# A two-layer trunk with a mixture of experts: the scatter moved into each expert, in four row tiles, and a shorter TensorE program for groups without second token blocks

## The reference

```
g_p, g_idx = top_k(softmax(x @ wg + bg), 1)
e_in       = logits of the 8 experts of that group
top_v, top_i = top_k(e_in, 2);  gate = g_p * softmax(top_v)
for expert e and its tokens:      # w1, w3: (1024, 512), w2: (512, 1024), float32
    a = silu(xb @ w1[e]) * (xb @ w3[e])
    y[tokens] += (a @ w2[e]) * gate
```

## Time and profile before

| | |
|---|---|
| runs | 1131.81, 1134.48, 1135.38 us |
| profiled execution | 1131.81 us, span 1130.0 us |
| mean granted TensorE clock | 0.928 of full |
| busy: PE, PEld, DVE, ACT | 880.1, 511.3, 345.5, 232.5 us |
| HBM read over the span | 423.85 MB, 376 GB/s |
| the chain that ended last | DMA 44%, PE 41%, DVE 7%, issue 5%, ACT 2% |

### The profile page before, as it was taken

How to read it: one execution, slowest core, us unless ns; L and a number is a source line. 1 busy time by engine, 2 the same in 40 slices (tenths; PEclk the granted TensorE clock), 3 DMA queues, 4 the chain that set the end, 5 groups by cost and what they waited for, 6 DMA issues and landing times.

```text
span 1130.0 us, 19738 instructions
## 1 busy us (share of the span) xinstructions
PE 880.1 (78%) x8032; PEld 511.3 (45%) x8033; DVE 345.5 (31%) x821; ACT 232.5 (21%) x559; POOL 4.6 (0%) x14
## 2 busy tenths in 40 slices
PE   6878777677786778589999988787887676768766
PEld 5644434333443344344886554443544343334433
DVE  2523222321322223222366253231332222213314
ACT  2421111110211111112144322110221121102112
POOL 1000000000000000000000000000000000000000
PEclk9899989998998989899999999999998898989979
DMA  9999999999999999998405459999999999999992
GB/s 299 428 424 424 425 426 425 423 427 425 426 425 426 425 426 426 425 425 358 176 1 200 166 208 426 425 426 413 426 426 425 425 426 425 428 423 425 427 426 112
DMA packets 33478, 427.19 MB, mean 378 GB/s; under 512 B 4706, under 2 KB 5986, under 8 KB 7988
## 3 DMA queue, kind: packets, MB, share of 16 engines
q1 hardware_dynamic: 33028, 424.19, 89.2%
q0 software_dynamic: 304, 0.72, 0.4%
HBM read 423.85 MB, written 1.05 MB: 376 GB/s over the span
## 4 chain that ended last, share of the span: by engine, by line
DMA 44%; PE 41%; DVE 7%; issue 5%; ACT 2%; DVEq 0%; SPq 0%
DMA ring<-in_moe_w 43%; PE ps L457 14%; PE ps L493 6%; PE ps L631 5%; PE ps L510 3%; PE ps L613 2%; DVE work L1061 2%; PE ps L411 2%; PE ps L685 2%; PE ps L363 1%; DMA work<-in_consts 1%; DVE work L1069 1%; ACT work L791 1%; PE ps L389 1%; DVE work L1063 1%
## 5 line engine op out<-in xcount | busy, mean ns | idle before, releaser
L457 PE MATMUL ps<-ring,work 128*32 128x256 f32 x4224 | 298.2, 434 | 164.8 <-DMA ring<-in_moe_w 100.7
L457 PEld LDWEIGHTS ps<-ring,work 128*32 128x32 f32 x4224 | 165.8, 124 | 304.7 <-issue 210.0
L1059 DVE TENSOR_SCALAR work<-work 128x128 f32<-128x128 f32 (+1 forms) x64 | 14.6, 229 | 501.3 <-ACT work L791 501.3
L493 PE MATMUL ps<-ring,work 128*32 128x256 f32 x2112 | 127.5, 382 | 30.8 <-DVE work L1069 30.2
L411 PE MATMUL ps<-work,h_sb 128*128 128x256 f32 (+1 forms) x576 | 136.2, 380 | 4.5 <-issue 3.8
L1095 DVE COPY hT<-ps 32x512 f32<-32x512 f32 x128 | 87.4, 683 | 149.0 <-PE ps L493 148.1
L791 ACT ACTIVATE work<-ps 128x256 f32<-128x256 f32 x64 | 24.5, 383 | 510.2 <-PE ps L457 510.2
L411 PEld LDWEIGHTS ps<-work,h_sb 128*128 128x128 f32 x576 | 99.6, 190 | 42.8 <-issue 32.9
L493 PEld LDWEIGHTS ps<-ring,work 128*32 128x32 f32 x2112 | 62.9, 109 | 92.9 <-DVE work L1069 44.9
L799 ACT COPY hT<-ps 32x512 f32<-32x512 f32 x128 | 73.9, 577 | 123.6 <-PE ps L493 122.9
L764 ACT ACTIVATE work<-ps,gcol 128x256 f32<-128x256 f32 (+1 forms) x144 | 58.6, 458 | 110.7 <-PE ps L411 110.7
(11 more groups left out here) (146 smaller groups left out, 420.8 us busy)
## 6 DMA issues: line engine op xcount, KB each, us to landing
ring<-in_moe_w SPq DMA_DIRECT2D x192, 2048.0 KB, 30.4
ring<-in_attn_wv SPq DMA_DIRECT2D x2, 2048.0 KB, 33.0
ring<-in_attn_wq SPq DMA_DIRECT2D x2, 2048.0 KB, 32.0
ring<-in_attn_wk SPq DMA_DIRECT2D x2, 2048.0 KB, 34.0
ring<-in_attn_wo SPq DMA_DIRECT2D x2, 2048.0 KB, 37.1
x_sb<-in_x SPq DMA_DIRECT2D x2, 512.0 KB, 5.7
work<-in_pool_w SPq DMA_DIRECT2D x1, 1024.0 KB, 13.0
out_x<-h_sb SPq DMA_DIRECT2D x2, 512.0 KB, 2.6
```

The costliest lines, as they stand in the source:

```text
L457: mm = pe.matmul(gu_ps[SB * j:SB * (j + 1), b, :, :], xg[:, u, kt, b, k, :], w[:, :, kt, P * j:P * (j + 1)], start=(kt == 0 and b == 0), s ...
L493: mm = pe.matmul(y_ps[SB * i:SB * (i + 1), b, :], actT[:, b, SB * j:SB * (j + 1)], w[:, j, 256 * i:256 * (i + 1)], start=(j == 0 and b == ...
```

## The change

The scatter is done after each expert's down products, by eight products per block: 32 rows deep (one expert's tokens stand in four copies, one for each quarter of the 1024 columns, at the partitions where the down products put them), 256 columns wide, four row tiles of PE, each with its own PSUM bank. `y` is then copied whole (128x256 for each block), by VectorE alone, and the gates are spread fourfold and transposed for each expert. The result lies in the banks by quarters of the columns, so that the residual is one instruction of 1024 columns for each half of the tokens. Banks of layer 1's first transposes and value products are moved, with which two waits of the queries go.

For each group TensorE now reads the largest count of tokens first and takes one of two programs: one for groups with no second block, without any branch within, and one as before. For the first group of a round the short one stands first, for the second group the long one.

More of the change, by code:

```diff
@@ L64 @@
 C_ALL = C_BAND + len(WINDOWS) * BW
-FILL_LAST = 1
 FILL_NEXT = 3
@@ L436, in group, with blocks_of_group @@
             def group(s, g, u, placed, rounds, fullest, tokens, chunk):
+                most = fullest()
[11 more added lines that the diff above has]
+                        blocks_of_group(s, g, u, placed, rounds, 1, lambda k: None, chunk)
+            def blocks_of_group(s, g, u, placed, rounds, blocks, tokens, chunk):
                 def second_block(count, step):
+                    if blocks == 1:
+                        return
                     if count is None:
@@ L1077, in group @@
                 ve.wait_ge(s["onehot"], placed)
-                for t in range(TH):
-                    ins = ve.tensor_tensor(gated[:, t, :, :, :], onehot[:, u, t, :, :, :],
-                                           W[:, t, bass.ds(gl * E4, E4)].unsqueeze(1).unsqueeze(3).to_broadcast([P, NB, E4, SB]),
-                                           ALU.mult)
-                ins.then_inc(s["gated"], 1)
                 for k in range(E4):
                     n1 = g * E4 + (k + 1)
+                    for t in range(TH):
+                        ins = ve.tensor_tensor(gated[:, t, :, :, :],
+                                               onehot[:, u, t, :, k, :].unsqueeze(2).to_broadcast([P, NB, 4, SB]),
+                                               W[:, t, bass.ds(gl * E4 + k, 1)].unsqueeze(1).unsqueeze(3)
+                                               .to_broadcast([P, NB, 4, SB]), ALU.mult)
+                    ins.then_inc(s["gated"], 1)
                     count = tokens(k)
@@ L1121, in experts, with residual @@
                                     group(fb, m * NGRP + g, g, u, m * (NGRP + 1) + g + 1, lambda k: None, lambda k: 0)
-                                    ve.wait_ge(fb["sc"], ACC * (m * NGRP + g + 1))
-            def residual(t, done, before):
+                                    ve.wait_ge(fb["sc"], E4 * (m * NGRP + g + 1))
+            def residual(t):
                 for i in range(2):
-                    ve.wait_ge(done, before + 2 * t + i + 1)
+                    ve.wait_ge(s_wo, 2 * t + i + 1)
                     xs = x_sb[:, t, 512 * i:512 * (i + 1)]
@@ L1163, in _ @@
             for t in range(TH):
-                residual(t, main["sc"], ACC * (NGRP - 1))
+                expert_residual(0, t)
                 copy_hT(1, t)
@@ L1241, in _ @@
             for t in range(TH):
-                residual(t, s_wo, 0)
+                residual(t)
                 copy_hT(2, t)
@@ L1248, in _ @@
             for t in range(TH):
-                residual(t, main["sc"], ACC * (2 * NGRP - 1))
+                expert_residual(1, t)
             for t in range(TH):
```

52 lines of the change are left out of this document (16 added, 36 removed).

## The result

| | before | after |
|---|---|---|
| median | 1133.22 us (4 runs) | 1146.37 us (1143.88 to 1146.85, 4 runs) |
| ratio, 95% interval | | 1.0114 [1.0102, 1.0126] |
| profiled execution, span | 1131.81, 1130.0 | 1146.15, 1144.3 |
| mean granted TensorE clock | 0.928 | 0.903 |

The direction and the range of the forecast (1140, 1129 to 1152) were right; the loss is twice as large as forecast: 14.3 us from profile to profile, where the sum has 7. The page after, against the earlier trace rows: slices of the span, instruction queue, gate products.

The account below looks back on a forecast made before the run. DMA was taken to bound the expert streams. The terms -2.2 - 1.4 + 10 + 0.5 + 0.1 = +7 gave 1138.8 us from the profiled execution, 1141.5 from the median; forecast 1140, range 1129 to 1152.

Parts of the forecast that it names:

- What bounds it: Expert streams: DMA at mostly 425 or 426 GB/s sets the time, hiding TensorE while it frees ring slots soon enough.
- the three open places: Where time is not hidden: end of layer 0, the very end, and start of layer 1, with DMA standing still.
- End of layer 0: Wait for the last scatter before attention: value products start at 508.9 against 511.06, a gain of 2.2 us.
- The end: Last scatter and first residual of the kernel: residual done at 1120.0 against 1121.41, a gain of 1.4 us.
- The ninth expert: Layer 1, behind the group with second blocks: two fetches, gate products end at 795.5, queue stands still 10 us longer.
- Other boundaries: Remaining group ends: double jumps fit, TensorE keeps 6.7 us per iteration; cost 0.5 us, bounds 0 and 8.
- the third rival: Short iterations: both holes follow every jump, TensorE becomes the bound, 10 to 15 us more, 1153 us; chance 0.12.
- The first rival: Group ends: jumps are free or hidden, only the ends move, -4.3 us, 1130.2 us; chance 0.15.
- The second: After the long group: one fetch instead of two, or a well placed piece boundary; hole 4 to 5 us, 1135; chance 0.18.

Follow-up runs that it names:

- e10: Changed kernel with eight never-executed products, a load and a branch ahead of layer 1's expert loop, shifting its code some 2 KB: 1140.99 us, 1.0072.
- e2: Kernel before with only the two programs per group, the scatter still once per group: 1133.92 us, 1.0008.
- e1: Changed kernel without the two programs per group, so only the scatter per expert is left: 1137.49 us, 1.0040.
- e8: Changed kernel with two programs for the first group of a round alone; the second always has the one with branches: 1139.58 us, 1.0057.
- e7: e2 with one more product of zeros (512 columns) behind the down products of every expert: 1134.61 us, 1.0015.
- e6: Kernel before with 16 more products per expert behind a branch never taken, fetched but not executed: 1136.52 us, 1.0035.
- e9: Changed kernel loading only half of each layer 1 weight chunk: a round takes 109 us against 116.9 to 117.6; no kernel time given.
- e11: Kernel before with one decision per layer; a layer without second blocks runs its own loop of short programs: 1131.16 us, 0.9981.
- e13: e11 with the last gather products and five products of zeros ahead of the branch choosing layer 0's program: 1133.24 us, 0.9996.

## Why the prediction was right in kind and half in size

- *What bounds it* held: the rate in the stream, the three open places, and the ring that has nothing in hand at the start of layer 1.
- *End of layer 0, -2.2.* The scatter took 1.15 us (1.07 forecast), the residual 1.22 (1.4), the value products started at 509.46 (508.9). But the gain did not arrive in the profiled execution: the granted clock was 0.92 in 505 to 510 and 0.74 in 510 to 515, after TensorE had stood idle for 1.33 and 0.83 us around eight short transposes, and the first 24 records cost 1.55 us more. Attention started at 539.88 against 539.94. E10, with the same code there, kept 1.00 and took 10.54, so this is one execution's, not a cost in each; its attention started at 538.63, 1.3 us earlier. The 1.7 us by which layer 1 starts earlier have nearly the size of this term, but by e2 another source: that the account closes here is luck. E1 has a second debit that my step did not have: its last chunk of layer 0 comes later, for a reason that stays open. The changed kernel doesn't show it, 499.52 against 499.04.
- *The end, -1.4.* 1.45. Right.
- *The ninth expert, +10.* The gate products ended at 796.6 (795.5 forecast), the queue lost 11.3 more than before. Right, with the mechanism: e1, without jumps, has no hole, and e8, with one jump of the pair, has half. The holes did not stay as two: one of 13.21 us, and then gate products of 6.43 instead of 3.66, since the clock had fallen to 0.50 (1.2 GHz) in the idle time. Some luck is in the closeness: layer 1 started 1.5 us later than forecast and the cycle is longer, but the single jump before it took 14.1 us from scatter to gate end, not 17.3.
- *Other boundaries, +0.5.* **This is the term that failed; it measured 5.1**, within my bounds of 0 and 8, at the thirteenth expert. I had written 59.1 us for a group ending in a double jump, against 59.2 of DMA. The layout of the sum left 0.1 us in hand, and I took it for enough. It was 64.8: the expert's cycle is 10.14 instead of 9.8 (three times 0.34), and the double jump 31.5 from gate end to gate end, where my sum has 26.9 (4.8 + 0.5 + 21.6). Those 4.6 us are the second hole, a piece that ends three records behind the target; e10 took it away and the time fell by 5.4. From term to term, the forecast's 7.0 and 0.5 (start of layer 1) + 1.3 (ninth expert) + 4.6 (here) + 1.0 (small dips) are the 14.3 measured. I knew of such holes from before's x1 record at 775.68, and put them into the bounds and the third rival, not into the sum.
- *The first rival* (free jumps) is out: every jump over a program took 5.8 to 7.2 us, wherever it stood. (The Trainium skill, Runtime: NRT & Kernel Launch, Instruction fetch mechanics, gives TensorE 128 KiB of instruction memory; no run here shows that the far side of such a jump was held.) *The second* (one fetch) is out by the hole of 13.21 us, twice that of e8's single jump. *The third*, TensorE as the bound because both holes follow every double jump, was half right: in layer 1 they do, 31.5, 30.8 and 30.3 us, in layer 0 they don't, 24.7 to 26.7. Since the loop's jump is 19.6 in layer 1, a round of short groups takes 116.5 to 117.6 there, just below 118.3. So TensorE gains about 1 us per round on the DMA, and does not hold it.
- The size of each part alone was misjudged in e2 and e7, both because I added costs that share one reserve, and because moving code changes the price of a jump by 5 to 6 us.

## What to carry to other kernels

A far jump is not a price per jump but a claim on whatever reserve the ring has at that place: lay TensorE's time from release to release beside the DMA's, group by group, and look for the group that starts with nothing in hand. Branches that save instructions are worth little where the stream hides TensorE, and cost jumps; code that is never executed isn't free either (e6, 3.7 us). Before believing a difference under 1% in a kernel whose loops fetch their code anew each round, shift the code by a few dozen instructions and time it again.

## What the runs showed of the hardware

- The same double jump, with the same work around it, took 25 or 31 us by the code's place alone (e10 and the changed kernel). In e10 the break moved to the loop's jump. It stands after 3, 13, 20, 33 or 38 records in the timelines of layer 1 here; in e7's layer 1 the gate products behind the far jumps have none.
- A far branch was 5.8 to 7.6 us in the changed kernel, whose DMA is nearly always full; in e9 4.0 to 4.6 while the DMA stood nearly still, and mostly 5.4 to 6.2 with chunks moving.
- Each hole costs more than itself: after 13 us without products the granted clock is 0.50, and 64 records take 4.9 to 6.5 us instead of 3.66 in the changed kernel and e10. A wait of 3.5 us was enough for 5.35 us (e11, e13).
- 16 pieces of code that is never executed made the kernel 3.7 us slower (e6), six times what their bytes take of the DMA (16*16.4 KB / 425 GB/s = 0.6 us). How is open; TensorE waiting for the code itself is likely a part.
- Four 32-row tiles, each with its own bank, ran side by side: 16 records of 256 columns in 1.15 us.
